# A last weight tile in two token halves, and the first tiles behind a norm block by block: a two-layer model on one core

## The reference, cut to what matters

```python
def rmsnorm(x, g):
    y = x * lax.rsqrt(jnp.mean(x * x, axis=-1, keepdims=True) + 1e-6)
    return y * g

# end of the token mixer, start of the channel mixer
x = x + rmsnorm(merged @ w_out, g_mix_post)          # "norm 1"
h = rmsnorm(x, g_ffn_pre)                            # "norm 2"
a = causal_dwconv(h @ w_gate, w_conv, b_conv)        # 3 taps along the tokens
y = (gelu(a) * (h @ w_up)) @ w_down                  # width 2816
x = x + rmsnorm(y, g_ffn_post)                       # "norm 3"
# start of the second block's attention
hn = rmsnorm(x, attn_norm)                           # "norm 4"
proj = hn @ w_in_2                                   # q, k, v, forget gate, fox gate
```

## Time and profile before

| | |
|---|---|
| median of 3 runs | 1532.11 us (1531.55 to 1532.72) |
| the profiled execution | 1531.17 us, of it the span 1529.4 us |
| PE busy | 1477.4 us, 97% of the span |
| DVE, ACT, POOL busy | 54%, 40%, 18% |
| mean granted TensorE clock | 0.993 of full speed |
| DMA | 128 MB, a mean of 84 GB/s |

### The profile page before, as it was taken

How to read it: one execution, slowest core, us unless ns; L and a number is a source line. 1 busy time by engine, 2 the same in 40 slices (tenths; PEclk the granted TensorE clock), 3 DMA queues, 4 the chain that set the end, 5 groups by cost and what they waited for, 6 DMA issues and landing times.

```text
span 1529.4 us, 23541 instructions
## 1 busy us (share of the span) xinstructions
PE 1477.4 (97%) x9287; PEld 1273.2 (83%) x9287; DVE 823.8 (54%) x1211; ACT 606.7 (40%) x922; POOL 278.6 (18%) x275
## 2 busy tenths in 40 slices
PE   7989999999979999999997999999999999999998
PEld 7989999999969988888885676888887888888887
DVE  5878645457374543553455546666756534334344
ACT  5542676642342221231233335556544413223230
POOL 2560333300016513540542000000100000000000
PEclk9999999999999999999998999999999999999999
DMA  5212111233203232222232222111122322223221
GB/s 195 70 57 83 57 56 61 78 114 108 98 28 97 90 102 83 96 96 96 83 106 87 69 84 70 42 42 42 42 95 86 109 96 96 97 88 104 84 98 66
DMA packets 35702, 128.30 MB, mean 84 GB/s; under 512 B 4068, under 2 KB 4196, under 8 KB 35488
## 3 DMA queue, kind: packets, MB, share of 16 engines
q1 hardware_dynamic: 34464, 122.18, 23.8%
q10 hardware_dynamic: 864, 4.33, 0.7%
q0 software_dynamic: 288, 0.57, 0.1%
HBM read 124.92 MB, written 2.10 MB: 83 GB/s over the span
## 4 chain that ended last, share of the span: by engine, by line
PE 77%; DVE 10%; ACT 7%; POOL 4%; issue 2%; DMA 0%; SPq 0%; DVEq 0%; ACTq 0%; POOLq 0%
PE ps L1749 67%; PE ps L2142 2%; DVE w_lo L879 1%; PE ps L1773 1%; POOL phase_tmp L1599 1%; ACT w_hi L372 1%; PE ps L2118 1%; PE ps L2129 1%; DVE rot L883 1%; ACT conv_tap L474 1%; DVE h_lo L892 1%; DVE x L892 1%; PE ps L2084 1%; DVE rot L1107 1%; POOL acc L1599 1%
## 5 line engine op out<-in xcount | busy, mean ns | idle before, releaser
L1749 PE MATMUL ps<-h_hi,w_hi 128*128 128x258 f32 (+2 forms) x1760 | 506.0, 337 | 33.2 <-DVE h_lo L892 18.3
L1749 PE MATMUL ps<-h_lo,w_hi 128*128 128x258 f32 (+2 forms) x1760 | 489.9, 328 | 0.0
L1749 PE MATMUL ps<-h_hi,w_lo 128*128 128x258 f32 (+2 forms) x1760 | 489.4, 328 | 0.0
L879 DVE TENSOR_TENSOR w_lo<-w_raw,w_hi 128x1024 fp32r<-128x1024 f32 (+2 forms) x226 | 291.3, 1290 | 209.7 <-ACT w_hi L372 208.9
L1749 PEld LDWEIGHTS ps<-h_hi,w_hi 128*128 128x128 f32 x1760 | 299.3, 190 | 86.4 <-issue 32.0
L1749 PEld LDWEIGHTS ps<-h_lo,w_hi 128*128 128x128 f32 x1760 | 297.2, 190 | 31.8 <-issue 4.4
L1749 PEld LDWEIGHTS ps<-h_hi,w_lo 128*128 128x128 f32 x1760 | 297.5, 190 | 30.2
L372 ACT ACTIVATE w_hi<-w_raw 128x1024 fp32r<-128x1024 f32 (+3 forms) x227 | 232.2, 1032 | 202.3 <-PE ps L1749 201.8
L1749 PE MATMUL ps<-mlp_lo,w_hi 128*128 128x512 f32 x256 | 100.9, 394 | 0.0
L1749 PE MATMUL ps<-mlp_hi,w_hi 128*128 128x512 f32 x256 | 100.3, 392 | 0.0
L1749 PE MATMUL ps<-mlp_hi,w_lo 128*128 128x512 f32 x256 | 99.4, 388 | 0.0
(11 more groups left out here) (310 smaller groups left out, 1873.7 us busy)
## 6 DMA issues: line engine op xcount, KB each, us to landing
w_raw<-w_units SPq DMA_DIRECT2D x227, 512.0 KB, 3.3
x<-x_t ACTq DMA_DIRECT2D x1, 2112.0 KB, 7.8
out<-out_tile SPq DMA_DIRECT2D x8, 256.0 KB, 2.0
x<-x_t ACTq DMA_DIRECT2D x3, 528.0 KB, 8.8
x<-x_t ACTq DMA_DIRECT2D x2, 264.0 KB, 4.3
consts<-consts SPq DMA_DIRECT2D x1, 320.0 KB, 6.5
b_step<-ssm_b SPq DMA_DIRECT2D x1, 256.0 KB, 10.1
c_step<-ssm_c SPq DMA_DIRECT2D x1, 256.0 KB, 10.9
```

The lines of the kernel that those rows point to most:

```text
L879: Dv.do(v.tensor_tensor(wlo[:, s % RING, 0:w], raw[:, s % RING, 0:w], f32(whi[:, s % RING, 0:w]), ALU.subtract), lo_ready)
L1749: ins = mm(o, wt[:, s % RING, w], xt[:, kx, c0:c0 + n], start=(b == 0 and a == 0), stop=(b == len(blocks) - 1 and a == 2))
```

## The change

Three things are changed, at norm 1 and at norm 3 alike.

- **The last unit in front of a post norm** (`last_unit`) runs over one half of the tokens first and over the other half then. Between the two, PE makes the sums of the first half. ACT now squares the other seven tiles as they are evacuated, and the last one by halves; the scaling, root and refinement are done half by half (`half_rstd`, `half_rsqrt`), each on 258 or 256 columns. The split of the third unit behind the norm is moved ahead of the first half's root on ACT and DVE.
- **The first two units behind it** (`two_units`) run together: for each block the hi parts of both (waiting for `h_hi` alone), then the sum of squares, then the low part of both. `residual` is in another order: the product and `x` of the next tile stand ahead of `h_lo` of this one.
- **The third unit** (`U_FFN + 2`, `U_V2 + 2`) writes banks 6 and 7 (or 6), so it waits for no evacuation.

Some loops of two trips are written out for this, and some semaphores elsewhere in the kernel are merged under shared names.

```diff
+            def half_square(norm, n, hf, src):            # ACT
+                act.wait_ge(sem("sq_added"), 6 * POST.index(norm) + KT - 3)
+                A.do(dn.activation(sq[1][:, hf * n // 2:(hf + 1) * n // 2], src, ACT.Square), sem("sq_half"))
-            with A.loop(2, {hi_ready: 4}) as i:
-                for j in range(4):
-                    split_hi(U_OUT + j + LOOK, i * 4)
-            squares(1, lambda m: ysum[:, m, 0:TW], lambda m: act.wait_ge(evacuated, U_OUT + m + 1))
-            rsqrt(1, TW)
+            for m in range(KT):
+                split_hi(U_OUT + m + LOOK)
+                if m:
+                    act.wait_ge(evacuated, U_OUT + m)
+                    post_square(1, m - 1, ysum[:, m - 1, 0:TW])
+            last = 2 * ((U_FFN - 1) % 2)
+            act.wait_ge(sem("half_mm"), 1)
+            half_square(1, TW, 0, PS[:, last, 0:TH])
+            split_hi(U_FFN + 2)
+            half_rsqrt(1, TW, 0)
+            act.wait_ge(unit_done, U_FFN)
+            half_square(1, TW, 1, PS[:, last + 1, 0:TH])
+            half_rsqrt(1, TW, 1)
...
+            def half_rstd(norm, n, hf):                   # DVE
+                c = slice(hf * n // 2, (hf + 1) * n // 2)
...
+                ts(rs[:, c], PS[:, 4 + hf, 0:n // 2], 1.0 / D_MODEL, EPS, M, A_, sem("ms_ready" if hf else "ms_a"))
...
+                newton(rs[:, c], acc[:, c], sq[0][:, c], rs[:, c], sem("rs_ready") if hf else None)
...
+            split_lo(U_FFN + 1)
+            split_lo(U_FFN + 2)
+            half_rstd(1, TW, 0)
+            for hf in range(2):
+                dve.wait_ge(sem("sq_half"), hf + 1)
+                Dv.do(v.tensor_copy(ysum[:, KT - 1, hf * TH:hf * TH + TH], PS[:, 2 * ((U_FFN - 1) % 2) + hf, 0:TH]),
+                      evacuated if hf else None)
+            half_rstd(1, TW, 1)
+            def residual(gain, n, c0, ready, hi, lo, pre):
...
+                for m in range(KT):
+                    Dv.fence()
+                    stt(x[:, m, c0:T1], ysum[:, m, 0:n], col(gain, m), x[:, m, c0:T1], M, A_, sem(ready))
+                    if m < KT - 1:
+                        tt(ysum[:, m + 1, 0:n], ysum[:, m + 1, 0:n], rs[:, 0:n], M)
+                    if m:
+                        low(m - 1)
+                low(KT - 1)
...
+            def last_unit(norm, n, s, xhi, xlo, outs, blocks):      # PE
+                j, h = POST.index(norm), n // 2
+                begin(s)
+                unit(s, 0, xhi, xlo, outs[0:1], None, 0, blocks, done=sem("half_mm"))
+                pe.wait_ge(sem("sq_added"), 6 * (j + 1))
+                for hf in range(2):
+                    mm(PS[:, 4 + hf, 0:h], ones, acc[:, h * hf:h * hf + h], start=True, stop=False)
+                pe.wait_ge(sem("sq_half"), 2 * j + 1)
+                mm(PS[:, 4, 0:h], ones, sq[1][:, 0:h], start=False, stop=True).then_inc(sem("stat_a"), 1)
+                unit(s, 0, xhi, xlo, outs[1:2], None, 0, blocks)
+                pe.wait_ge(sem("sq_half"), 2 * j + 2)
+                mm(PS[:, 5, 0:h], ones, sq[1][:, h:n], start=False, stop=True).then_inc(sem("stat_mm"), 1)
+            def two_units(s, outs, hi, lo, after):
+                begin(s)
+                begin(s + 1)
+                for k in range(KT):
+                    w = slice(k * P, k * P + P)
+                    pe.wait_ge(sem(hi), k + 1)
+                    for q in range(2):
+                        for a, wt in enumerate((whi, wlo)):
+                            for o, c0, n in outs[q]:
+                                mm(o, wt[:, (s + q) % RING, w], hhi[:, k, c0:c0 + n], start=(k == 0 and a == 0), stop=False)
+                    after(k)
+                    pe.wait_ge(sem(lo), k + 1)
+                    for q in range(2):
+                        for o, c0, n in outs[q]:
+                            ins = mm(o, whi[:, (s + q) % RING, w], hlo[:, k, c0:c0 + n], start=False, stop=(k == KT - 1))
...
+                    if s0 + 2 * q == U_FFN + 2:
+                        pe.wait_ge(lo_ready, U_FFN + 3)
+                        unit(U_FFN + 2, 0, hhi, hlo, late_halves(U_FFN + 2, 6, 0))
...
+            two_units(U_V2, [[(PS[:, (U_V2 + j) % 2, :], 0, SEQ)] for j in range(2)], "h3_hi", "h3_lo",
+                      lambda k: tile_sum(4, SEQ, k))
+            pe.wait_ge(lo_ready, U_V2 + 3)
+            unit(U_V2 + 2, 0, hhi, hlo, [(PS[:, 6, :], 0, SEQ)])
+            v2_transposes(0)
```

More of the change, by code:

```diff
@@ L1244, in _ @@
                        f32(hhi[one].rearrange("p a b -> p (a b)")), S_, sem("mg_lo"))
-            with Dv.loop(2, {lo_ready: 4, evacuated: 4}) as i:
-                for j in range(4):
-                    split_lo(U_OUT + j + LOOK, i * 4)
-                    dve.wait_ge(unit_done, i * 4 + (U_OUT + j + 1))
-                    Dv.do(v.tensor_copy(two(ysum[:, bass.ds(i * 4 + j, 1), 0:TW].rearrange("p a b -> p (a b)")),
-                                        late((U_OUT + j) % 2)), evacuated)
@@ L1253, in residual @@
-            def residual(norm, gain, n, c0, ready, hi, lo, pre):
-                rstd(norm, n)
-                for m in range(KT + 1):
-                    if m < KT:
-                        tt(ysum[:, m, 0:n], ysum[:, m, 0:n], rs[:, 0:n], M)
-                    if m:
-                        dve.wait_ge(sem(hi), m)
-                        stt(hlo[:, m - 1, 0:n], x[:, m - 1, c0:T1], col(pre, m - 1), f32(hhi[:, m - 1, 0:n]), M, S_, sem(lo))
-                    if m < KT:
-                        Dv.fence()
-                        stt(x[:, m, c0:T1], ysum[:, m, 0:n], col(gain, m), x[:, m, c0:T1], M, A_, sem(ready))
+            for m in range(KT - 1):
+                split_lo(U_OUT + m + LOOK)
+                dve.wait_ge(unit_done, U_OUT + m + 1)
+                Dv.do(v.tensor_copy(two(ysum[:, m, 0:TW]), late((U_OUT + m) % 2)), evacuated)
@@ L1737, in _, with unit @@
             mm = nc.tensor.matmul
-            def unit(s, r, xhi, xlo, outs, ready=None, base=0, blocks=None, last_of_unit=True, after=None):
+            def unit(s, r, xhi, xlo, outs, ready=None, base=0, blocks=None, last_of_unit=True, after=None, done=unit_done):
                 blocks = blocks or [(k, k) for k in range(KT)]
@@ L2031, in _ @@
                 s0 += 2 * tiles
+                if f0 + tiles == FFN_TILES:
+                    break
                 with pe.Fori(0, 2) as i:
```

162 lines of the change are left out of this document (107 added, 55 removed).

## The result

| | before | after |
|---|---|---|
| median of 4 runs, one chip | 1531.83 us (1530.86 to 1532.72) | 1523.68 us (1523.19 to 1524.16) |
| the profiled execution, of it the span | 1531.17, 1529.4 us | 1523.19, 1521.4 us |

The ratio is 0.9946, with a 95% interval of 0.9934 to 0.9957: 8.15 us less, where 9.4 were forecast. The time lies inside the forecast's own range of 1520.5 to 1525. The two spans are 8.0 us apart, and that is the sum that can be followed row by row.

What follows compares the result with a forecast made beforehand. PE was taken to bound the kernel nearly everywhere, except at the post norms, where it idles or is fed too slowly. Gains of 2.4 (norm 1) and 7.0 (norm 3) sum to 9.4 us, giving 1522.7; own range 1520.5 to 1525.

Steps and rivals of the forecast that it cites:

- clock loss at norm 1: After PE's return at norm 1: half of 4.5 us at the lower clock is lost work, 2.25 us.
- S, the eighth sum: End of the last block's sum of squares in the joined units: 454.0 at norm 1, 851.7 at norm 3.
- gain kept from norm 1: At the fifth unit behind norm 1: start at 468.4 instead of 470.78, a gain of 2.4 us.
- gain at norm 3: At the fifth unit behind norm 3: start at 865.05 instead of 872.08, a gain of 7.0 us.
- The chain to the first `x`: Half unit to first `x`: 432.3 at norm 1, 1.1 us earlier; 830.7 at norm 3, 3.1 us earlier.
- signs of being wrong: PE waiting for `h_hi` or `h_lo` mid-units, clock at 0.50 beyond 5 us after PE's return, or first `x` no earlier.
- What takes part of it back: Behind norm 1's S: PE waits 0.4 us at the fourth unit and 2.1 more at the fifth, for its split.
- From there on PE is the bound again and nothing changed, so it is kept: Behind the fifth unit after norm 3: the summed gain of 9.4 us stays to the end.
- The clock doesn't fall: Rival at PE's two norm waits: clock stays up or falls at one only; 4.0 us less, 1518.7; chance 0.12.
- The halves bring nothing: Rival before both norms: half rounds as long as whole ones, only 5.2 us gained, 1526.9; chance 0.16.
- Absorbed later: Rival later in the kernel: PE waits for weight transfers or POOL's key bias, gain lost, 1532.1; chance 0.05.
- Slower: Rival in the joined units: finer waits keep PE at the lower clock through both stretches, 1555.3; chance 0.05.

Runs made afterwards that it cites:

- split5: The change with the split of `U_FFN + 4` moved ahead of the first gelu on ACT and right behind the first `up` evacuation on DVE: 1520.26 us, ratio 0.9923.
- warm5: The change with two matmuls of constants on PE in its wait at the fifth unit behind norm 1: 1522.18 us, ratio 0.993.
- n1_only: The change at norm 1 alone, norm 3 and what follows as before except the value tiles' first turns, one unit later: 1529.17 us, ratio 0.998.
- warm: The change with four matmuls of constants on PE in each wait for the first `h_hi`, behind both norms: 1519.01 us, ratio 0.9914.

## Why the prediction was right, step by step

| step | predicted | measured |
|---|---|---|
| first `x` at norm 1 | 432.3 | 432.50 |
| PE's return | 433.85 | 434.16 |
| block of the two units | 2.3 | 2.29 |
| clock loss at norm 1 | 2.25 | about 2.7 |
| S, the eighth sum | 454.0 | 454.44 |
| fifth unit | 468.4 | 468.77 |
| gain kept from norm 1 | 2.4 | 2.0, of which 0.5 kept (in these two executions) |
| first `x` at norm 3, less the gain by then (0.5) | 830.2 | 830.25 |
| PE's return at norm 3, same | 831.7 | 831.90 |
| S at norm 3, same | 851.2 | 850.85 |
| fifth unit behind norm 3, same | 864.55 | 864.10 |
| gain at norm 3 | 7.0 | 7.5 |

**The chain to the first `x`.** Summing instruction by instruction gave both starts within 0.2 us. At norm 1 PE's last sum ends at 429.40, and DVE scales it at 429.47; the prediction had 429.4 for both. At norm 3 DVE waits 1.24 for the second half's sum at 827.24; the prediction's sum has this as half square and half sum, 0.45 + 0.7.

**The joined units.** PE is the bound there with 2.29 a block, and the waits are gone, as predicted. The lower level cost more than its term at norm 1: from 434.16 to about 439.6, 5.5 us and 2.7 of work, for 2.25. At norm 3 it lasted 3.7 us, 1.85 of work, for 1.75. With PE's return, 0.3 late, this makes S late by 0.4 at norm 1. It is also one of the prediction's own signs of being wrong: the clock was to be at 0.50 for at most 5 us behind PE's return, and at norm 1 it was for 5.5. The mechanism stands, but that limit was set from the 4.5 and 3.5 us of one trace, and the nine profiles without constants in these waits range from 2.9 to 6.1. That the two terms came within 0.5 of this profile is partly luck.

**What takes part of it back.** PE was to wait 2.1 at the fifth unit behind norm 1, on the split behind the gelu; it waited 1.95, and split5 shows that this split is the cause. The wait of 0.4 at the fourth unit isn't in the trace: it starts at 461.00, S + 6.56, where the prediction had S + 6.7.

**The step that failed** is the sentence "From there on PE is the bound again and nothing changed, so it is kept". A wait was added, and behind a wait the clock can fall. It took 1.5 of norm 1's 2.0 in the profiled execution, and warm5 gives the same 1.5 in medians; n1_only's median leaves room for less in other executions. The prediction priced the clock at the two long waits alone, where before had shown it, and not at the one that it forecast itself. The forecast less this term, plus the 0.5 at norm 3, less the 0.4 at norm 1, is 9.4 - 1.5 + 0.5 - 0.4 = 8.0, the difference of the spans. So the time lies in the range because the one term left out is smaller than the range is wide, and because norm 3 gave a little more than forecast.

**The rivals.** *The clock doesn't fall*: false here, and its price of 4.0 was 4.7 (warm). *The halves bring nothing*: half right. At norm 3 they cost 1.2, the split's place included, and the earlier squares bring more than the whole gain; the prediction named both causes for norm 3 ("since ACT's squares and POOL's additions no longer come after the last unit"), but took a half round as useful in both places. At norm 1 the halves bring 0.9. *Absorbed later*: not by transfers or POOL; a part was, by the clock. *Slower*: the clock stayed at 1.00 from 440 to the fifth unit, so PE's block by block work doesn't pull it down. The Trainium skill, "TensorE: Matmul & The Clock Gate", section "A second HAM failure mode: psum-queue depth-cycling", as the prediction read it, would have had it swing there; in no trace here does it swing while PE is fed in small steps without a wait of a microsecond or more.

## What to carry to other kernels

When a stretch is shortened, follow the next four or five units down every queue: what fed PE in time before (here a weight split behind a gelu, and a pair of banks that came free late) is what it waits for next, and it decided about 7 (the banks) and 3.4 us (the split) here, against 8.15 for the whole change. Halving the last unit in front of a norm has to win more than the second round of small instructions adds, and what is moved between the halves stands on the chain: read the distance from the last full evacuation to the first output for both forms. Where PE has to wait, give it constants to multiply: two lines brought 4.7 us at two waits, and about 1.5 at a third. And when a price is taken from two medians or two traces, look first whether the clock did the same in both in places that no edit touched.
